# Two transformer blocks on one core: the feed forward in one stage, LayerNorm sums taken beside the out products, the norm's end by chunks in the next stage, ple in one stage

## The reference

```
def layer_norm(x, g, b):
    mu = jnp.mean(x, -1); var = jnp.mean(jnp.square(x - mu), -1)
    return (x - mu) * lax.rsqrt(var + LN_EPS) * g + b
def swiglu(h, w_in, w_out):                       # w_in 1024 x 5632, w_out 2816 x 1024
    gate, up = jnp.split(h @ w_in, 2, axis=-1)
    return (jax.nn.silu(gate) * up) @ w_out
def first_block(...):
    for i in range(DEPTH):                        # DEPTH = 2
        h = layer_norm(ALPHA * h + 0.5 * swiglu(h, ffa_w_in[i], ffa_w_out[i]), ...)
        h = layer_norm(ALPHA * h + hybrid_mixer(h, ...), ...)
        h = layer_norm(ALPHA * h + 0.5 * swiglu(h, ffb_w_in[i], ffb_w_out[i]), ...)
        h = h + jax.nn.sigmoid(h @ ple_w_gate[i]) * (p[i] @ ple_w_proj[i])   # p[i]: 512 x 256
```

## Time and profile before

| | |
|---|---|
| median of 3 runs | 4107.07 us (4103.67 to 4107.86) |
| the profiled execution | 4095.71 us |
| its span | 4093.9 us |
| mean granted clock of TensorE | 0.938 of full |
| busy PE, DVE, ACT, POOL | 3633.7, 1768.6, 1217.7, 437.7 us |
| DMA | 324.02 MB, mean 79 GB/s |

### The profile page before, as it was taken

How to read it: one execution, slowest core, us unless ns; L and a number is a source line. 1 busy time by engine, 2 the same in 40 slices (tenths; PEclk the granted TensorE clock), 3 DMA queues, 4 the chain that set the end, 5 groups by cost and what they waited for, 6 DMA issues and landing times. The chain is left out here.

```text
span 4093.9 us, 49349 instructions
## 1 busy us (share of the span) xinstructions
PE 3633.7 (89%) x19466; PEld 2763.6 (68%) x19466; DVE 1768.6 (43%) x2376; ACT 1217.7 (30%) x1703; POOL 437.7 (11%) x422
## 2 busy tenths in 40 slices
PE   7999898888999699989979699977999797869997
PEld 6878564666877478767738488755787575347876
DVE  5532354545532365323555455223332356643322
ACT  3221433233221332223332322224322233233221
POOL 0000112520001000010034100011000200330001
PEclk9999898999999899999989899988999899879998
DMA  4332110013331134212200133212222122012221
GB/s 152 139 115 82 62 62 23 3 42 113 138 110 55 63 139 147 96 61 73 66 7 4 47 139 140 99 42 70 93 97 95 59 74 63 15 47 87 92 98 56
DMA packets 88124, 324.02 MB, mean 79 GB/s; under 512 B 12648, under 2 KB 14696, under 8 KB 87536
## 3 DMA queue, kind: packets, MB, share of 16 engines
q1 hardware_dynamic: 87920, 321.21, 23.3%
HBM read 319.06 MB, written 2.12 MB: 78 GB/s over the span
## 5 line engine op out<-in xcount | busy, mean ns | idle before, releaser
L214 DVE TENSOR_TENSOR w_low<-w_raw,w_high 128x1024 fp32r<-128x1024 f32 (+2 forms) x496 | 632.0, 1276 | 1497.4 <-ACT w_high L209 1497.0
L209 ACT ACTIVATE w_high<-w_raw 128x1024 fp32r<-128x1024 f32 (+2 forms) x496 | 543.6, 1098 | 1450.7 <-PE ffa_in_ps L228 265.5
L226 PE MATMUL ffa_in_ps<-ffa_x_high,w_high 128*128 128x512 f32 x704 | 281.7, 400 | 39.4 <-DVE ffa_x_low L271 39.4
L226 PE MATMUL f_in_ps<-b_f_x,w_high 128*128 128x512 f32 x704 | 282.8, 402 | 22.6 <-DVE b_f_x L359 21.5
L226 PE MATMUL ffb_in_ps<-ffb_x_high,w_high 128*128 128x512 f32 x704 | 281.6, 400 | 23.5 <-DVE ffb_x_low L271 23.5
L227 PE MATMUL ffa_in_ps<-ffa_x_low,w_high 128*128 128x512 f32 x704 | 280.4, 398 | 0.0
L228 PE MATMUL f_in_ps<-b_f_x,w_low 128*128 128x512 f32 x704 | 280.3, 398 | 0.0
L227 PE MATMUL f_in_ps<-b_f_x,w_high 128*128 128x512 f32 x704 | 280.3, 398 | 0.0
L227 PE MATMUL ffb_in_ps<-ffb_x_low,w_high 128*128 128x512 f32 x704 | 279.9, 398 | 0.0
L228 PE MATMUL ffa_in_ps<-ffa_x_high,w_low 128*128 128x512 f32 x704 | 279.6, 397 | 0.0
L228 PE MATMUL ffb_in_ps<-ffb_x_high,w_low 128*128 128x512 f32 x704 | 279.2, 397 | 0.0
(11 more groups left out here) (492 smaller groups left out, 6792.2 us busy)
## 6 DMA issues: line engine op xcount, KB each, us to landing
w_raw<-in_ffa_in SPq DMA_DIRECT2D x88, 512.0 KB, 5.1
w_raw<-in_ffb_in SPq DMA_DIRECT2D x88, 512.0 KB, 4.5
w_raw<-in_ffn_in SPq DMA_DIRECT2D x88, 512.0 KB, 3.3
w_raw<-in_mix_in SPq DMA_DIRECT2D x80, 512.0 KB, 3.5
w_raw<-in_ffa_out SPq DMA_DIRECT2D x32, 704.0 KB, 4.0
w_raw<-in_ffb_out SPq DMA_DIRECT2D x32, 704.0 KB, 4.1
w_raw<-in_ffn_out SPq DMA_DIRECT2D x32, 704.0 KB, 4.1
ffa_in_ada_raw<-in_w_ada SPq DMA_DIRECT2D x36, 512.0 KB, 3.5
```

The lines of the kernel that those rows point to most:

```text
L209: act.activation(self.high[:, half, :kt * P], self.raw[:, slot, :kt * P], ACT.Copy).then_inc(self.rounded, 1)
L214: dve.tensor_tensor(self.low[:, half, :kt * P], self.raw[:, slot, :kt * P], self.high[:, half, :kt * P].bitcast(F32), ALU.subtract).then_i ...
L226: pe.matmul(out, w_high, x_high[:, k0 + k, :], start=start and k == 0, stop=False)
```

## The change

1. **One stage for a feed forward** (`feed_forward`): 44 in blocks and 16 out blocks in one stage, four PSUM banks in turn for both.
2. **One weight stream for the program**: the layers are written out in Python in place of the loop, nothing is cleared, loads run four blocks ahead and rounding and split one block ahead across stages.
3. **LayerNorm about an early mean.** After `early` chunks their mean (the origin) is taken off: later chunks have it subtracted from the state before they are added to, earlier ones after. Squares (ACT) and sums (POOL) of the centred chunks are made beside the products. Behind the last product come only the matmuls by ones of the last chunks, then variance = mean of squares - mean squared. rstd and shift = mean * rstd are left in a tile `norm`; the state isn't normed yet.
4. **`NormHalves`**: the next stage (mixer's in, second feed forward, ple) does by chunk: DVE times rstd, POOL minus shift, ACT gain and bias, ACT high half, DVE low half. PE does the first two weight blocks in turn by halves of four chunks (`multiply_first`), in the second block's stages too.
5. **ple in one stage**: six projection blocks ahead, kept in PSUM, then gates with the last two projections between; the norm's end is in it.
6. In `out_proj` the table load stands ahead of the input's split, and the first block's rounding in the stage before.

```diff
 class WeightStream:
-    def load(self, sp, between=None):
-        source, count = self.matrices[self.at]
...
+    def load_upto(self, sp, g):
+        while self.n_loaded <= min(g, len(self.blocks) - 1):
+            n, (source, kt) = self.n_loaded, self.blocks[self.n_loaded]
+            at_least(sp, self.split, n - SLOTS + 1)
...
+    def round_upto(self, act, g):
+        while self.n_rounded <= min(g, len(self.blocks) - 1):
+            n, cols = self.n_rounded, self.blocks[self.n_rounded][1] * P
+            act.wait_ge(self.landed[n % SLOTS], 16 * (n // SLOTS + 1))
+            at_least(act, self.used, n - HALVES + 1)
...
+class NormHalves:
+    LAG = 2
+    def gpsimd(self, pool):
+        for k in range(KD):
+            pool.wait_ge(self.scaled, k + 1)
+            pool.tensor_tensor(self.h[:, k, :], self.h[:, k, :], self.shift, ALU.subtract).then_inc(self.shifted, 1)
+    def scalar(self, act, x_high):
+        for k in range(KD):
+            act.wait_ge(self.shifted, k + 1)
+            act.activation(self.h[:, k, :], self.h[:, k, :], ACT.Identity, scale=self.gain[:, k:k + 1],
+                           bias=self.bias[:, k:k + 1]).then_inc(self.done, 1)
+            act.wait_ge(self.done, k + 1)
+            act.activation(x_high[:, k, :], self.h[:, k, :], ACT.Copy).then_inc(self.rounded, 1)
+    def vector(self, dve, x_high, x_low):
+        for k in range(KD + self.LAG):
+            if k < KD:
+                dve.tensor_tensor(self.h[:, k, :], self.h[:, k, :], self.rstd, ALU.mult).then_inc(self.scaled, 1)
+            if k >= self.LAG:
+                j = k - self.LAG
+                dve.wait_ge(self.rounded, j + 1)
+                dve.tensor_tensor(x_low[:, j, :], self.h[:, j, :], x_high[:, j, :].bitcast(F32), ALU.subtract)\
+                    .then_inc(self.ready, 1)
...
+def multiply_first(pe, ws, g, banks, x_high, x_low, ready):
+    for part in (range(0, KD // 2), range(KD // 2, KD)):
+        for j in range(2):
+            ws.multiply(pe, g + j, banks[j], x_high, x_low, True, True, ready=ready if j == 0 else None, part=part)
...
-def ffn_in(nc, ws, name, x_high, x_low, halves, hidden_high, hidden_low, small=(), modulation=None):
+def feed_forward(nc, ws, name, halves, finish, norm, small=(), modulation=None):
...
             @block.scalar
             def _(act):
+                ws.round_upto(act, first + 1)
+                halves.scalar(act, x_high)
...
+                for n in range(blocks):
+                    ws.round_upto(act, first + n + 1)
+                    if 0 < n <= IN_BLOCKS:
+                        activate(n - 1)
+                    if n == IN_BLOCKS:
+                        act.preload_act_table_set(EXP_LN)
+                    if n >= IN_BLOCKS:
+                        finish.scalar_beside(act, n - IN_BLOCKS)
+                finish.scalar(act)
...
 class LayerNorm:
+    def scalar_beside(self, act, j):
+        if j == self.origin_after + 1:
+            act.wait_ge(self.origin_done, 1)
+            act.activation(self.origin[:, :], self.p_origin[:, :], ACT.Copy, scale=-1.0 / (self.early * P))\
+                .then_inc(self.origin_ready, 1)
+        for m in self.squares_at.get(j, ()):
+            self.take_square(act, m)
+    def tensor(self, pe):
+        for m in range(self.last_added + 1, KD):
+            self.wait_final(pe, m)
+            mean = pe.matmul(self.p_mean[:, :], self.ones, self.h[:, m, :], start=False, stop=m == KD - 1)
+            if m == KD - 1:
+                mean.then_inc(self.mean_done, 1)
+            pe.wait_ge(self.squared, m + 1)
+            var = pe.matmul(self.p_var[:, :], self.ones, self.square[:, m % self.RING, :], start=False, stop=m == KD - 1)
+        var.then_inc(self.var_done, 1)
+def feed_forward_norm(h, norm, const):
+    return LayerNorm(h, 0.5, norm, const, early=4, moved_first=4, last_added=6, origin_after=8, parts_after=14,
+                     squares_at={10: (0, 1), 11: (2, 3), 12: (4,), 13: (5,), 14: (6,)})
+def mixer_norm(h, norm, const):
+    return LayerNorm(h, 1.0, norm, const, early=2, moved_first=3, last_added=5, origin_after=2, parts_after=KD - 1,
+                     squares_at={5: (0, 1), 6: (2, 3, 4), 7: (5,)})
...
 def ple(...)
             @block.scalar
             def _(act):
+                ws.round_upto(act, first + 1)
                 act.wait_ge(p_landed, 16)
                 split_high(act, p_rounded, p_high, p, KP)
+                halves.scalar(act, x_high)
+                for n, (of_gate, m) in enumerate(order):
+                    ws.round_upto(act, first + n + 1)
+                    if of_gate:
+                        act.wait_ge(ws.used, first + n + 1)
+                        at_least(act, added, m - 1)
+                        act.activation(gate[:, m % 2, :], ps[m % 2][:, :], ACT.Sigmoid).then_inc(gated, 1)
...
-            with nc.Fori(0, DEPTH) as layer:
-                first_layer(nc, ws, h, m, const, {k: v[layer] for k, v in t.items() if k in LAYERED}, first,
-                            mod, c_silu, layer)
+            for layer in range(DEPTH):
+                with ExitStack() as own:
+                    first_layer(nc, ws, h, m, const, layers[layer], own, mod, c_silu, layer, norm)
```

More of the change, by code:

```diff
@@ L172, in load @@
-    def load(self, sp, between=None):
-        source, count = self.matrices[self.at]
[L176 to L222, removed]
+        self.blocks, self.first = [], 0
+        self.n_loaded = self.n_rounded = self.n_split = 0
+    def begin(self, blocks):
+        self.blocks = blocks
+    def claim(self, count):
+        self.first += count
+        return self.first - count
+    def load_upto(self, sp, g):
+        while self.n_loaded <= min(g, len(self.blocks) - 1):
+            n, (source, kt) = self.n_loaded, self.blocks[self.n_loaded]
+            at_least(sp, self.split, n - SLOTS + 1)
+            sp.dma_start(self.raw[:, n % SLOTS, :kt * P], source).then_inc(self.landed[n % SLOTS], 16)
+            self.n_loaded += 1
@@ L223, in multiply @@
+    def multiply(self, pe, g, out, x_high, x_low, start, stop, k0=0, ready=None, part=None):
+        kt = self.blocks[g][1]
+        ks = range(kt) if part is None else part
+        pe.wait_ge(self.split, g + 1)
+        for k in ks:
             if ready is not None:
                 pe.wait_ge(ready, k0 + k + 1)
-            w_high, w_low = (w[:, half, k * P:(k + 1) * P] for w in (self.high, self.low))
+            w_high, w_low = (w[:, g % HALVES, k * P:(k + 1) * P] for w in (self.high, self.low))
@@ L473, in out_proj @@
+                finish.tensor(pe)
+def out_proj(nc, ws, name, x, finish):
+    n_ps = 4
+    first = ws.claim(KD)
     with ExitStack() as ctx:
-        ps = [ctx.enter_context(nc.psum_tensor(f"{name}_ps{j}", [P, S], F32)) for j in range(chunks)]
+        x_high, x_low = (ctx.enter_context(nc.sbuf_tensor(f"{name}_x_{n}", [P, KD, S], F32R)) for n in ("high", "low"))
+        ps = [ctx.enter_context(nc.psum_tensor(f"{name}_ps{j}", [P, S], F32)) for j in range(n_ps)]
         finish.allocate(nc, ctx, name)
-        with stage(nc, name, ["x_rounded", "x_ready", "taken", *finish.names]) as (
-                block, x_rounded, x_ready, taken, *sems):
+        with stage(nc, name, ["x_rounded", "x_ready", "taken", *finish.names]) as (block, x_rounded, x_ready, taken, *sems):
+            finish.signals(taken, *sems)
```

687 lines of the change are left out of this document (345 added, 342 removed).

## The result

The changed kernel took 3997.28 us (median of 4, 3995.05 to 4001.79) beside 4105.37 for the kernel before; the ratio is 0.9742, 95% interval 0.9727 to 0.9757. The forecast was 4002. The two profiled executions took 4095.71 and 3996.81 us, with spans of 4093.9 and 3994.9: the sum of the parts is made against this difference of 99.0, not against the medians' 108.

What follows compares the result with a forecast made beforehand. TensorE, busy 89% (3633.7 of 4093.9 us), bounds the kernel; its stops at stage borders can come back. Terms summed to -106.5, taken as -105: 4107 - 105 = 4002 us, with 3966 to 4044 expected 8 times in 10.

Steps and rivals of the forecast that it cites:

- In to out: Border between a feed forward's in and out products, six times: idle 38.9 us and cold products 13.1 go, -52.
- the pace of 2.27 by exclusion: Norm's end in the next stage: POOL and DVE don't overlap, so one chunk costs 1.12, 0.55 and 0.60: 2.27 us.
- A: Border into the mixer, last product before to the 49th behind: 34.1 us instead of 41.77, twice, -15.3.
- B: Border into the second feed forward, last product before to the 49th behind: 35.3 us instead of 38.42, twice, -6.3.
- C1: Stretch over ple into layer 1, to its 49th product: 112.3 us instead of 126.55, -14.3.
- C2: Stretch over ple into the second block, to the 49th product: 131.4 us instead of 143.78, -12.4.
- G: Start of an output projection to its 49th product: 15.85 us instead of 19.91, first block rounded earlier; three times, -12.3.
- Ones matmuls: The norm's sums by ones among the products: 14 pairs at 1.1 us, +15.
- Start: Program's start: a second rounding of 1.06 us, against which turns of two blocks fill waits; estimate -1.2.
- Faster halves: Rival, chance 0.10: chunk phases go at 1.4 us instead of 2.27; 30 us more come back, 3972.
- Slower halves: Rival, chance 0.15: halves run slower, PE cold behind them; 23 to 52 us less gained, 4025 to 4054.
- The slower case: Rival, chance 0.03: squares waiting for POOL's moves delay weight roundings; six norms each cost over 17.5 us, 105 together.

Runs made afterwards that it cites:

- experiment 2: The changed kernel with each feed forward again as two stages with a barrier between, first out block still rounded ahead: span 4027.3 us, ratio 0.9823 to the kernel before.
- experiment 4: The changed kernel with the norm's subtraction by chunk moved from POOL to DVE: span 3987.7 us, ratio 0.9727 to the kernel before.
- experiment 1: The changed kernel with the norm whole again behind the last out product, the next stage only splitting: span 4003.8 us, ratio 0.9794 to the kernel before.
- experiment 3: The changed kernel with the first two weight blocks multiplied one behind the other, not in turns: span 4028.6 us, ratio 0.9821 to the kernel before.
- experiment 8: The changed kernel run once more, unaltered: span 3995.2 us, ratio 0.9743 to the kernel before.
- experiment 6: The changed kernel with POOL adding chunk 6 too in the mixer's norm, four ones matmuls behind the last product, not six: span 4004.6 us, ratio 0.9767.

## Why the prediction was right

**The borders.** In to out was right as a sum, and experiment 2 splits it. Its two reasons, idle time and the cold start, were read from the earlier trace rows, and with the barrier the idle time came back at all six borders and the cold start at four.

**The chunk phase.** The step that was least sure, the pace of 2.27 by exclusion, measured 2.29, and A, B, C1 and C2 came within 1 us each. The Trainium skill (GPSIMD Engine Reference, Key points) names the contention of GpSimd with VectorE operations that have two SBUF inputs; the trace agrees, by 1.76 us instead of 0.69 for such an operation. In experiment 4, without POOL, the pace is 1.93. But for A and B the forecast was right with less room than it seemed. I had the last low half set the end. In the changed kernel it does, just so: at A in layer 0 PE waits for it,

```profile
433.33 0.69 DVE L308 TENSOR_TENSOR mix_x_low<-state,mix_x_high 128x512 fp32r<-128x512 f32 x1 [0.99 <-ACT mix_x_high L299]
...
434.08 0.50 PE L192 MATMUL mix_proj_ps<-mix_x_high,w_high 128*128 128x512 f32 x1 [0.58 <-DVE mix_x_low L308]
```

and at the other three borders of A and B PE starts on the last chunk 0.06 to 0.26 us behind that half, without a wait. PE's own work ends at the same time: it does its first products cold, at A in layer 0 0.427 apart until 429.3, in the second block's first half. Experiment 4 brought the last half 3.5 us forward, PE then started on that chunk 1.3 to 2.3 us behind it, and the end moved by 1.4 to 2.4 only. That both meet was luck; no term of the sum had PE's own end. The tail ahead of it was right too (404.55 to 411.01 is 6.46), though its written terms add up to 6.35 and not to 6.45.

**ple.** The sum for C1 held in its parts, too: 6.6 us to the stage, 87.2 to the last gate product (forecast 86.7), 18.6 from there to layer 1's 49th product (forecast 19.05). The third block's rounding begins 1.9 us earlier than forecast.

**The norm.** Against a norm kept whole the early mean nearly cancels: it gives some 7 us at each A, 3 and 5 at B and 1 at ple, 24 in all, and pays 12 in the stream. The prediction didn't draw this sum; the expectation of experiment 1 did, at 12, and the run gave 8.9 by its span.

**Mis-sized terms.** The sum of the forecast was 106.5 and its stretches measured 99.0; G alone is the difference, the others cancel. That the medians lie 108 apart, and the forecast of 4002 is 5 us off, owes something to luck. *Ones matmuls*: 12.0, not 15; among products one costs 0.85, since only the pace counts there and not the 1.13 of an isolated pair. *G*: 4.6, not 12.3. The mechanism was right: 16.57 us from the stage's start instead of 19.91, -3.3 where I had 4.1; in the second block all of the 3.3 is left. What took it back in the mixers is PE's clock in the stretch ahead of it. The same window before was

```profile
637.99:877.99 240.00, 190.92 (x3082) 137.37 (x3081) 126.39 (x264) 76.22 (x141) 86.96 (x79) 0.89 0.04 11
```

and without G's own part it went from 220.1 us to 223.0, with PE busy 177.8 and 180.6: the same instructions, 2.8 more of busy time, 2.9 more of length. Experiment 4's two layers show the same: PE is busy 189.7 us in the one (234.6 long, clock 0.90) and 197.7 in the other (241.6, 0.86). Why the clock differs there is open. *Start*: +1.0 instead of -1.2. The second rounding of 1.06 was counted; the gain from turns isn't to be seen where halves come every 0.55 us. Experiment 3 has the start 0.4 shorter without them, but so has the unaltered kernel in experiment 8, so what turns do there is not shown. *The program's tail* is 1.6 shorter, and only 0.6 in the second trace of the same kernel. The clearing of the weight stream's semaphores stood there, which I had left out; that it is the cause was not tried.

**The rivals.** Faster halves fell at the first trace (2.29). Slower halves too. The slower case had its mechanism right and its place wrong: POOL can hold up a norm, but the mixer's, not the feed forward's, and by a late sum behind the last product, not by a rounding. The mixer's norm has not even two additions to spare (experiment 6), and with POOL's work doubled it costs 15 us each, not 105 in all.

## What to carry to other kernels

Take a change of many parts apart before building on it: removing the barrier and taking turns on PE brought 30 us each for a few lines, the rewritten norm 9 to 21 for most of the code. Where a stage's activation queue is one written order, look at what stands ahead of the first weight rounding that PE waits for; moving six roundings in each ple gave 21 us. When DVE and POOL share a chain with operations of two SBUF inputs, put their times one behind the other, as here (1.14, 0.55 and 0.60 for three of them), before hoping for overlap. And run the unaltered kernel twice before a microsecond in one stretch is laid to an edit.

## What the runs showed of the hardware that I had not expected

- POOL and DVE took turns so exactly that a DVE multiplication of 0.69 us lasted 1.75 to 1.78 beside a POOL subtraction, and ended 0.55 behind it, each of the 36 times that it began beside one.
- PE's granted clock differed in one and the same stretch. The last 192 products of ple took 46.4, 49.4 to 49.7, 50.9 or 52.5 us in different kernels, and 49.4 and 50.9 in two traces of the changed kernel. With two waits of 1.97 in them it was 49.4 to 52.5, at 0.93 to 1.00; with one wait of 1.16, 46.4 in both kernels that had it. That small shifts of time ahead of it decide is likely, but not shown: why the same two waits cost the clock in one trace and not in another is open.
- The mixer's middle, untouched by any edit, took 234.6 to 241.8 us, following the granted clock (0.90 to 0.86). A gain of 3 us in such a program can vanish into it, and is to be read from its own stretch.
